# Grouped-query attention: every second block of 512 queries takes two passes of p times v, with the maxima units and the remainders of p dealt out anew

## What is computed

```python
def _attend_queries(q, k, v, scale):
    s = jnp.einsum('bqhgd,bkhd->bhgqk', q, k, preferred_element_type=jnp.float32) * scale
    p = jax.nn.softmax(s, axis=-1).astype(v.dtype)
    return jnp.einsum('bhgqk,bkhe->bqhge', p, v)
```

## Time and profile before

| | us |
|---|---|
| median of 3 runs | 3897.84 (3897.72 to 3899.2) |
| the profiled execution | 3894.24 |
| its span, first to last instruction | 3892.3 |
| the eight GQA heads, first `qk` at 593.7 to first `qk` of head 8 at 1609.94 | 1016.2 |
| PE idle before the first `qk` of heads 1 to 8, in this order | 2.10, 2.24, 2.01, 3.34, 3.59, 2.23, 1.98, 2.63 |
| the eight MLA heads, to the last `pv_lo` | about 1035 |

### The profile page before, as it was taken

How to read it: one execution, slowest core, us unless ns; L and a number is a source line. 1 busy time by engine, 2 the same in 40 slices (tenths; PEclk the granted TensorE clock), 3 DMA queues, 4 the chain that set the end, 5 groups by cost and what they waited for, 6 DMA issues and landing times. The chain is left out here.

```text
span 3892.3 us, 53957 instructions
## 1 busy us (share of the span) xinstructions
PE 3599.2 (92%) x17079; PEld 2878.0 (74%) x17079; DVE 2776.8 (71%) x4984; ACT 2341.2 (60%) x4266; POOL 1221.9 (31%) x1105
## 2 busy tenths in 40 slices
PE   7999969999999999999999999998999389999991
PEld 7999946666766676788888888876888367777770
DVE  5666668888988898889888988864444655555553
ACT  4444406777777777777777777785333055555554
POOL 0000001011110111488888888891000023333320
PEclk9999969999999999999999999998999799999995
DMA  5465681332133213320332133003433088888877
GB/s 178 164 228 174 199 197 63 65 65 44 27 63 65 44 27 65 63 55 16 65 64 44 27 64 65 7 8 114 146 135 124 23 275 261 269 261 258 257 210 281
DMA packets 315271, 462.88 MB, mean 119 GB/s; under 512 B 120641, under 2 KB 251997, under 8 KB 303869
## 3 DMA queue, kind: packets, MB, share of 16 engines
q1 hardware_dynamic: 256468, 368.47, 32.3%
q0 software_dynamic: 19152, 69.74, 7.0%
q10 hardware_dynamic: 39456, 22.29, 1.9%
HBM read 313.38 MB, written 147.54 MB: 118 GB/s over the span
## 5 line engine op out<-in xcount | busy, mean ns | idle before, releaser
L997 POOL TENSOR_TENSOR b_p_lo<-b_prob,b_p_hi 128x512 fp32r<-128x512 f32 x704 | 916.9, 1313 | 782.5 <-ACT b_prob L1041 778.1
L1040 ACT ACTIVATE b_p_hi<-b_psS 128x512 fp32r<-128x512 f32 (+1 forms) x1376 | 824.4, 599 | 531.1 <-PE b_psS L1232 512.8
L1232 PE MATMUL b_psS<-b_q,b_k 96*128 96x512 f32 (+3 forms) x3440 | 1067.6, 408 | 25.3 <-DMA b_q<-b_nmxT 23.5
L1041 ACT ACTIVATE b_prob<-b_psS 128x512 f32<-128x512 f32 (+1 forms) x1376 | 818.2, 595 | 0.0
L1232 PEld LDWEIGHTS b_psS<-b_q,b_k 96*128 96x128 f32 (+3 forms) x3440 | 599.8, 184 | 189.4 <-DMA b_q<-b_nmxT 26.4
L1142 DVE TENSOR_REDUCE b_mx_s<-b_psM 128x1 f32<-128x412 f32 (+1 forms) x1228 | 679.4, 580 | 68.6 <-PE b_psM L1283 58.2
L1283 PE MATMUL b_psM<-b_k,b_q 96*128 96x412 f32 (+7 forms) x1596 | 558.4, 355 | 29.5 <-DMA b_q<-QGL 21.8
L1273 PE MATMUL b_psO<-b_p_lo,b_v 128*65 128x512 f32 (+1 forms) x1280 | 508.3, 397 | 0.4 <-POOL b_p_lo L997 0.4
L1110 DVE TENSOR_TENSOR b_p_lo<-b_prob,b_p_hi 128x512 fp32r<-128x512 f32 x576 | 418.8, 733 | 66.0 <-ACT b_prob L1041 58.1
L1125 DVE TENSOR_TENSOR b_acc<-b_acc,b_prob 128x512 f32<-128x512 f32 (+1 forms) x592 | 409.3, 691 | 45.6 <-ACT b_prob L1041 29.6
L1283 PEld LDWEIGHTS b_psM<-b_k,b_q 96*128 96x128 f32 (+1 forms) x1596 | 305.0, 191 | 139.0 <-DVE b_mx_s L1142 32.6
(11 more groups left out here) (256 smaller groups left out, 5758.4 us busy)
## 6 DMA issues: line engine op xcount, KB each, us to landing
e_w_gu<-w_gate SPq DMA_DIRECT2D x34, 1024.0 KB, 6.2
e_w_gu<-w_up SPq DMA_DIRECT2D x34, 1024.0 KB, 12.4
e_w_dn<-w_down SPq DMA_DIRECT2D x34, 1024.0 KB, 14.0
a_x_raw<-xallT SPq DMA_DIRECT2D x25, 512.0 KB, 5.1
a_x<-xall SPq DMA_DIRECT2D x25, 512.0 KB, 4.2
c_o<-O SPq DMA_DIRECT2D x24, 512.0 KB, 4.9
c_x<-xall SPq DMA_DIRECT2D x24, 512.0 KB, 3.2
H<-c_h SPq DMA_DIRECT2D x24, 512.0 KB, 2.6
```

Source lines behind the costliest of these rows:

```text
L997: nc.gpsimd.tensor_tensor(p_lo[:, slot, :], prob[:, slot, :], p_hi[:, slot, :].bitcast(F32), ALU.subtract).then_inc(lo_ready, 1)
L1040: nc.scalar.activation(p_hi[0:kn, slot, :], psS[0:kn, j % 2, :], ACT.Exp)
L1041: nc.scalar.activation(prob[0:kn, slot, :], psS[0:kn, j % 2, :], ACT.Exp).then_inc(p_ready, 1)
L1232: m = nc.tensor.matmul(psS[0:kn, j % 2, :], kk[s][0:r, k], qq[s][0:r, q], start=n == 0, stop=n == len(passes) - 1)
```

## The change

In GQA heads the blocks 0, 2 and 4 take the MLA form of p times v, the blocks 1, 3 and 5 keep theirs. `two(h, b)` says which form holds. In the blocks of two passes:

- `pv_hi` is one matmul, `pv_lo` one with both halves of v, and the meta item has one in place of two;
- the remainder of p of every item of keys is made on POOL;
- DVE sums `prob` into `acc`, three items behind;
- `o_turn` has the MLA form, and ACT's next use of a slot waits for that slot's sum.

In the blocks of three passes POOL makes two of three remainders, DVE those of the items with j % 3 == 1. In a GQA head 67 of the 80 remainders are then POOL's and 13 DVE's. The 104 units lie in the same 70 steps: one a step behind blocks of two passes, two behind blocks of three, one less in a busy step, and a third in eight of the steps; by rows of steps 0 to 16, 17 to 33, 34 to 50, 51 to 67 and 68 to 76 these are 10, 33, 18, 34 and 9 units, before 17, 24, 24, 24 and 15. A third unit stands behind `pv_lo`. MLA heads keep their order. Two scratch arrays and the array of ones shrink from 56 to 4 rows (`PAIRS` to `Q_PAIRS`).

```diff
+        def two(h, b):
+            return h >= GH or b % 2 == 0
+        def rest_on_pool(h, j):
+            return two(h, BLOCK_OF[j]) or not j % 3 == 1
+        def unit_steps(h):
+            steps = range(R, R + SPAN)
+            room = {}
+            for j in steps:
+                busy = j - NORM_AT in END_OF or j == R + NORM_AT - TURN_AT or META_ITEM[j - DEN_LAG]
+                room[j] = (1 if two(h, BLOCK_OF[j - DEN_LAG]) else 2) - busy
+            wide = [j for j in steps if room[j] == 2 and rest_on_pool(h, j - SPLIT_LAG)]
+            more = NU - sum(room.values())
+            if h < GH:
+                for k in range(more):
+                    room[wide[k * len(wide) // more]] += 1
+                return [j for j in steps for _ in range(room[j])]
...
@@ ACT
-                if not gqa:
-                    act.wait_ge(den_done, (h - GH) * NI + j + 1)
+                used = divmod(h * NI + j - NP, NI)
+                if used in SUMS:
+                    act.wait_ge(den_done, SUMS[used] + NP)
...
@@ DVE
+            def follow(n):
+                h, j = divmod(n - SPLIT_LAG, NI)
+                if 0 <= h < HEADS and (h, j) not in SUMS:
+                    split(h, h % 2, j)
+                h, j = divmod(n - DEN_LAG, NI)
+                if (h, j) in SUMS:
+                    den_add(h, h % 2, j)
...
@@ PE
-                if gqa:
+                if not two(h, b):
                     nc.tensor.matmul(psO[0:VD + 1, b % 2, :], v[s][:, vc, ROUNDED], p, start=first, stop=False)
                     nc.tensor.matmul(psO[0:VD, b % 2, :], v[s][:, vc, REST], p, start=False, stop=False)
                 else:
...
                     pv_hi(h, s, gqa, j - HI_LAG)
-                    for u in units[1:]:
+                    for u in units[1:2]:
                         unit_of(h, i1, s, nxt, u)
                     pv_lo(h, s, gqa, j - LO_LAG)
+                    for u in units[2:]:
+                        unit_of(h, i1, s, nxt, u)
```

More of the change, by code:

```diff
@@ L806, in stage_attend @@
         SPAN = 70
-        UNIT_AT = {}
-        calm = [j for j in range(R, R + SPAN) if j - NORM_AT not in END_OF and j != R + NORM_AT - TURN_AT
-                and ITEMS[j - DEN_LAG][2] != META]
-        for u in range(NU):
-            UNIT_AT.setdefault(calm[u * len(calm) // NU], []).append(u)
         FINISH_AT, ROW_AT = R + SPAN, R + SPAN + 3
-        POOL_EVERY = 8
         V_AT = {16: slice(8, 16), 22: slice(16, 24), 40: slice(0, 8)}
         META_ITEM = [kn == META for _, _, kn, _, _, _ in ITEMS]
-        NKEY = META_ITEM.count(False)
@@ L819, in stage_attend @@
-        ON_POOL = [j for j in range(24, NI - 3) if j % POOL_EVERY == 0 and not META_ITEM[j]]
-        POOL_GQA, DVE_GQA = len(ON_POOL), NKEY - len(ON_POOL)
-        def on_pool(gqa, j):
-            return not gqa or j in ON_POOL
-        def rest_of(h, j, gqa):
-            n = META_ITEM[:j].count(False) + 1
-            if not gqa:
-                return lo_ready, GH * POOL_GQA + (h - GH) * NKEY + n
-            before = sum(k < j for k in ON_POOL)
-            if j in ON_POOL:
-                return lo_ready, h * POOL_GQA + before + 1
-            return lo_ready_dve, h * DVE_GQA + n - before
+        HEADS = GH + MH
@@ new lines, in two @@
+        def two(h, b):
[14 more added lines that the diff above has]
+                return [j for j in steps for _ in range(room[j])]
+            calm = [j for j in steps if j - NORM_AT not in END_OF and j != R + NORM_AT - TURN_AT
+                    and not META_ITEM[j - DEN_LAG]]
+            return [calm[u * len(calm) // NU] for u in range(NU)]
@@ new lines, in stage_attend @@
+        UNITS_AT = {}
+        for gqa in (True, False):
+            steps = unit_steps(0 if gqa else GH)
+            assert len(steps) == NU
+            for u, j in enumerate(steps):
+                UNITS_AT.setdefault((gqa, j), []).append(u)
+        POOL_RESTS, DVE_RESTS, SUMS = {}, {}, {}
+        for h in range(HEADS):
+            for j in range(NI):
+                if not META_ITEM[j]:
+                    rests = POOL_RESTS if rest_on_pool(h, j) else DVE_RESTS
+                    rests[h, j] = len(rests) + 1
+                if two(h, BLOCK_OF[j]):
+                    SUMS[h, j] = len(SUMS) + 1
@@ L1101, in split @@
             def split(h, s, j):
-                if on_pool(True, j) and not META_ITEM[j]:
+                if not META_ITEM[j] and (h, j) not in DVE_RESTS:
                     return
@@ L1194, in _ @@
             dve.sem_inc(den_done, NP)
-            for j in range(R - SPLIT_LAG):
-                split(0, 0, j)
+            for j in range(R):
+                follow(j)
             def head(h, i, s, gqa, nxt, last):
                 for j in range(R, NI):
-                    follow(h, s, gqa, j - lag(gqa))
+                    follow(h * NI + j)
                     if not last:
-                        for u in UNIT_AT.get(j, ()):
+                        for u in UNITS_AT.get((gqa, j), ()):
                             unit(h + 1, u)
@@ L1212, in head @@
                 normalise(h, NB - 2, use(h, NB - 2, last), gqa)
-                for j in range(NI - lag(gqa), NI):
-                    follow(h, s, gqa, j)
-                if not last:
-                    for j in range(R - lag(nxt)):
-                        follow(h + 1, 1 - s, nxt, j)
-                else:
+                for j in range(NI, NI + R):
+                    follow(h * NI + j)
+                if last:
                     normalise(h, NB - 1, use(h, NB - 1, last), gqa)
@@ L1339, in head @@
                     qk(h, s, gqa, j)
-                    units = () if last else UNIT_AT.get(j, ())
+                    units = () if last else UNITS_AT.get((gqa, j), ())
                     for u in units[:1]:
```

33 lines of the change are left out of this document (13 added, 20 removed).

## The result

The changed kernel takes 4010.22 us (median of 4 runs, 4008.97 to 4023.06), the kernel before, beside it on the same chip, 3898.52 (3897.72 to 3902.82). The ratio is 1.029, with a 95% interval of 1.028 to 1.031: 2.9% slower, where I had forecast 1.4% faster, and outside my range of 3822 to 3882.

The account below looks back on a forecast made before the run. PE was taken to set the pace in the GQA heads. The terms -80.1 + 22.4 - 8 + 8 + 4 = -53.7 us gave 3840.5 from the profile, 3844 us against the median, 1.4% faster; range 3822 to 3882.

Parts of the forecast that it names:

- Matmuls removed, -80.1: GQA blocks 0, 2 and 4: 43 matmuls fewer in each of 8 heads, 0.233 us each, -80.1 us.
- turns added: Turning steps of GQA heads: 0.35 us more each, four of twelve hidden in the gap at the head's end, +22.4 us.
- DVE, +4: GQA heads: DVE loses 59 remainders, gains 43 sums; only eight three-unit steps a head are tight, 0.5 us a head, +4 us.
- decides from 0.56 us a remainder: Rival, three-pass blocks: DVE's 13 remainders wait for POOL's running one, up to +114 us, 3954 us; chance 0.07.
- The gap and the clock, -8: Ends of GQA heads: gap shrinks from 2.0-3.6 to 0.6-2.2 us; low clock behind it halfway gone, -8 us.
- POOL, +8: Two-pass blocks of GQA heads: POOL's lag behind PE mostly hidden by slack, 1 us a head, +8 us.
- POOL as the bound: Rival, two-pass blocks: no slack hides POOL's lag, +48 in place of +8 us, 3884 us; chance 0.15.
- ACT, 0: GQA heads: same exponentials, and the new wait for the sum of the item five before costs nothing.

Follow-up runs that it names:

- e2: The changed kernel with only the small meta remainders of GQA heads moved from DVE to POOL: 3920.8 us, ratio 1.0063.
- e3: The changed kernel with only DVE's 13 remainders of p a GQA head moved to POOL, meta ones left on DVE: 3965.83 us, ratio 1.0178.
- e4: The changed kernel with its 104 units spread over the steps as before the change: 3893.86 us, ratio 0.9996.
- e1: The changed kernel with all remainders of GQA heads, meta ones too, on POOL; units as changed: 3877.98 us, ratio 0.9956.
- e10: e7 with POOL's and ACT's parts of v moved to later steps and DVE copying the transposed maxima ahead of step 79's sum: 3867.47 us, ratio 0.9927.
- e11: e1 with each remainder of p in GQA heads made over 256 of 512 columns, output not the layer's: 3872.35 us, ratio 0.9923.
- e7: e1 with the units spread 13, 30, 20, 30, 11 by rows of steps, never three in a step: 3870.5 us, ratio 0.9933.
- e5: The changed kernel with DVE's remainders in GQA heads reading acc (PSUM) in place of prob (SBUF), output not the reference's: 3938.21 us, heads 1004.5.

## Why the prediction was wrong

By the steps of the prediction, in the heads: forecast 962, measured 1132.6.

- **Matmuls removed, -80.1, and turns added.** Both held as prices. A turning step in the three-pass block behind the transpose now goes from 1153.03 to 1154.65 = 1.62 us, where it was 1.27: the 0.35 us more that I had put there. What failed is that four of the twelve turns would vanish in the gap. See the third point.
- **DVE, +4: the step that failed, and with it the sign.** I had the mechanism and named it as a rival, with the condition "decides from 0.56 us a remainder". Three things were wrong with its size. First, I capped the wait at one POOL instruction (1.1 us), since that was the longest that the earlier trace rows shows; but in the GQA heads before POOL is busy 124 of 1016 us, and in MLA heads POOL kept up: where the meta remainder waited beside a run there, POOL's next input came only after DVE had begun to wait, and DVE was let in. Nothing in the trace of before showed what a run of 14 does, so its longest row was no bound. Second, I counted 13 instructions a head and left the six meta ones out of the price, though the earlier trace rows shows 1828 ns for them too: they cost 88 to 95 us, the 13 cost 39 to 46 (e2, e3). Third, I priced the wait of DVE alone, not the clock behind it. In numbers: PE waited 82.4 us for reductions in place of 4, and the low clock while PE was busy took 56.3 us in place of 15.9 - 8. That is 78 + 48 = 126 of the 171 us between forecast and measurement.
- **Why the runs exist** stood in my own sums. I had worked out that POOL falls behind by 2.6 to 3.8 us in block 0, called it hidden, and used it for POOL's price only. A lag of POOL is a run without gaps and with inputs in store, and at the end of that run, at the meta item of the next block, stands a DVE instruction with two inputs in SBUF, with units behind it. The two terms, which I had summed as independent, meet there. The change itself brought the condition about (e4).
- **The gap and the clock, -8: wrong.** The idle time at the ends of heads hardly shrank: 18.2 us over eight heads, and 19.6 in e1, against 20.1 before, where I had forecast 1.4 us less at each of eight ends. The extra 1.4 us of turns did go in there, but from the row transpose to the next scores it is now 11.1 to 12.7 us, where it was 10.1 to 10.4 in five heads and up to 11.7 in the others. In e4, with the same turns, it is 10.4 to 11.9 us and the idle time 11.1 us in all, so there the forecast of the gap held. One part of the longer way shows: block 4 now has a sum, and the copy of the transposed maxima stands behind it on DVE.

```profile
1148.44 0.27 PE L1306 MATMUL b_psT<-b_ident,b_nmx 128*24 128x128 f32 x1 [0.51 <-DVEq L1190]
...
1148.45 0.69 DVE L1143 TENSOR_TENSOR b_accS<-b_acc,b_prob 128x512 f32<-128x512 f32 x1 [0.20 <-issue]
1149.06 0.27 DVE L1172 CAST b_nmxT<-b_psT 24x128 fp32r<-24x128 f32 x1
...
1159.54 0.74 PE L1247 MATMUL b_psS<-b_q,b_k 128*128 128x512 f32 x2 [1.53 <-DMA b_q<-b_nmxT]
```

The transpose waits 0.51 us, and the copy starts 0.62 us after it. But e10, which takes the copy out from behind the sum, still has 10.9 to 12.6 us there, so most of what is new lies in the transfer itself. Why it takes longer in most variants and not in e4 is open.
- **POOL, +8: held, or up to twice that.** PE's matmuls waited 0.2 us for POOL by the profile and its weight loads 2.3 us a head, and e11 puts its pace at 1 to 2 us a head. The rival "POOL as the bound" (+48) is out.
- **ACT, 0: too low.** At the turn of block 1, which now falls among steps of two passes, PE waits for ACT's copy: L1316, 9.2 us in eight heads, before 1.3.
- **Without the DVE term**, the kernel that answers to my forecast is e1: 998.6 us of heads where I had 962, and a gain of 18 to 20 us in place of 54. Of the 37 us that are missing, 11 are the turns that the gap did not hide, 6 the clock that did not recover (15.3 for 8.9), 8 ACT's copy. POOL's pace was in the forecast with 8 and measured 8 to 16. The last 4 to 12 us I can't assign: steps with three units, whose weight loads still wait 22.6 us in 84 short pieces, are the likely place, and e7, which has none, is 10 us shorter in the heads. That was not tested apart.

**Who goes next.** The 152 instructions of e5 show that what matters is two inputs in SBUF, not the engine or the load, and so agree with the Trainium skill, "SBUF — State Buffer", section "SBUF: two separate sides", on which instructions exclude each other. The Trainium skill has the one that starts first hold the way for its whole length, and says nothing there of who is next. I read it as "at most one instruction of the other engine". The rows bear that out in 203 of 249 places (counted in the last section). In the other 46 POOL's next instruction went ahead of the one that waited, and up to four did so one after another.

## What to carry to other kernels

A DVE instruction with both inputs in SBUF can cost its own time plus what is left of POOL's run, and not of POOL's instruction alone, where POOL has inputs in store; before giving POOL more work, find where its queue falls behind and which such DVE instruction stands at that place, and what is queued behind it. Move that one to POOL too, however small it is, or give it an input from PSUM, or leave POOL gaps: each of the three took 115 to 134 us off these heads. And a sum of terms is only as good as the terms are independent: an engine that is "late but hidden" in one term is the condition of another.
